# Two-layer decoder with 64 routed experts: meta sums behind gate and up, shorter gathered rows, token lists handed out in two parts

## What is computed

```
scores  = sigmoid(x @ w_router)                      # 272 x 64
groups  = the best 4 of 8, by their two best biased scores
top_idx = the 8 best experts of those groups
gates   = scores[top_idx] / sum * 2.5
routed  = sum over the chosen experts e of gate * ((silu(x @ w_gate[e]) * (x @ w_up[e])) @ w_down[e])
shared  = (silu(x @ ws_gate) * (x @ ws_up)) @ ws_down
h       = layer_norm(alpha * h + routed + shared)
```

## Time and profile before

| | |
|---|---|
| median of 3 runs | 1403.47 us (1402.36 to 1405.37) |
| the profiled execution | 1402.51 us, its span 1400.7 us |
| PE busy | 1351.8 us (97%) |
| DVE, ACT, POOL busy | 429.9, 221.4, 350.7 us |
| DMA | 475.60 MB, mean 340 GB/s |
| chain that ended last | PE 78%, SPq 11%, DMA 4%, DVE 3% |

### The profile page before, as it was taken

One profiled execution on the slowest core, in us unless ns is written; L12 is line 12 of the kernel. 1 busy time (PEld: TensorE's weight loads), 2 busy tenths in 40 slices (PEclk: granted clock), 3 DMA queues, 4 the chain that ended last, 5 costly groups with the idle time before them and its releaser, 6 DMA issues.

```text
span 1400.7 us, 20398 instructions
## 1 busy us (share of the span) xinstructions
PE 1351.8 (97%) x7932; PEld 706.5 (50%) x7932; DVE 429.9 (31%) x1278; ACT 221.4 (16%) x547; POOL 350.7 (25%) x371
## 2 busy tenths in 40 slices
PE   8999999999999999999989999899999999999997
PEld 4755454454454454445448555455454545444443
DVE  0442562222322322222154424532223232222223
ACT  1154120101111111011021540101111011101001
POOL 2031435232232232232000212352222323222201
PEclk9999999999999999999999999999999999999999
DMA  9732378999999999999875224699999999999993
GB/s 338 309 120 78 135 252 319 423 419 419 422 422 419 422 422 422 420 421 421 339 261 192 85 99 155 253 393 420 422 418 422 421 421 419 421 422 421 420 424 153
DMA packets 92098, 475.60 MB, mean 340 GB/s; under 512 B 16292, under 2 KB 22744, under 8 KB 42752
## 3 DMA queue, kind: packets, MB, share of 16 engines
q1 hardware_dynamic: 76864, 442.73, 77.7%
q0 software_dynamic: 15168, 32.01, 6.3%
HBM read 491.21 MB, written 3.75 MB: 353 GB/s over the span
## 4 chain that ended last, share of the span: by engine, by line
PE 78%; SPq 11%; DMA 4%; DVE 3%; issue 2%; POOL 1%; ACT 1%; POOLq 0%; DVEq 0%; ACTq 0%
PE bank L636 24%; PE bank L666 13%; PE bank L613 13%; SPq L469 11%; PE bank L715 6%; PE bank L726 5%; PE bank L942 3%; DMA ring<-in_w_up_dram 2%; PE bank L837 2%; PE bank L654 1%; DMA arena<-h_rows,rank_i 1%; PE bank L609 1%; PE bank L985 1%; PE bank L818 1%; PE bank L586 1%
## 5 line engine op out<-in xcount | busy, mean ns | idle before, releaser
L1883 POOL DMA_INDIRECT arena<-h_rows,rank_i x256 | 255.7, 999 | 649.6 <-DVE arena L1551 504.9
L636 PE MATMUL bank<-ring,arena 128*64 128x256 f32 x2816 | 313.4, 379 | 12.9 <-DMA ring<-in_w_up_dram 9.4
L636 PEld LDWEIGHTS bank<-ring,arena 128*64 128x64 f32 x2816 | 203.8, 137 | 133.9 <-issue 28.0
L613 PE MATMUL bank<-arena 128*128 128x512 f32 x512 | 247.1, 606 | 0.0
L1584 DVE TENSOR_TENSOR arena<-arena,bank 128x256 f32<-128x256 f32 x64 | 26.9, 421 | 561.2 <-ACT arena L1153 561.2
L666 PE MATMUL bank<-ring,arena 128*64 128x512 f32 x704 | 160.8, 598 | 0.0
L1546 DVE STREAM_TRANSPOSE arena<-arena 128x256 f32<-128x256 f32 x256 | 141.5, 609 | 30.5 <-DMA arena<-h_rows,rank_i 27.0
L1158 ACT ACTIVATE arena<-bank 128x512 f32<-128x512 f32 x128 | 76.5, 598 | 440.4 <-PE bank L666 440.4
L636 PE MATMUL bank<-arena 128*64 128x256 f32 x1280 | 142.2, 379 | 3.8 <-DMA arena<-in_w_up_dram 3.8
L613 PEld LDWEIGHTS bank<-arena 128*128 128x128 f32 x512 | 87.7, 191 | 87.7 <-issue 86.7
L636 PEld LDWEIGHTS bank<-arena 128*64 128x64 f32 x1280 | 91.7, 137 | 59.4 <-issue 10.6
(11 more groups left out here) (213 smaller groups left out, 898.2 us busy)
## 6 DMA issues: line engine op xcount, KB each, us to landing
ring<-in_w_gate_dram SPq DMA_DIRECT2D x44, 2048.0 KB, 25.7
ring<-in_w_up_dram SPq DMA_DIRECT2D x44, 2048.0 KB, 27.8
ring<-in_w_down_dram SPq DMA_DIRECT2D x44, 2048.0 KB, 25.5
arena<-in_w_gate_dram SPq DMA_DIRECT2D x20, 2048.0 KB, 25.9
arena<-in_w_up_dram SPq DMA_DIRECT2D x20, 2048.0 KB
arena<-in_w_down_dram SPq DMA_DIRECT2D x20, 2048.0 KB, 25.6
ring<-in_w_in_dram SPq DMA_DIRECT2D x8, 2048.0 KB, 21.6
ring<-in_w_o_dram SPq DMA_DIRECT2D x4, 2048.0 KB, 11.6
```

Source lines behind the costliest of these rows:

```text
L613: last = mm(bank[SUM_BANKS[n][half]][0:w, :], selg[:, u, t0:t0 + w], y_sb[:, u, half * 512:(half + 1) * 512], start=False, stop=stop, skip ...
L636: last = mm(bank[5][64 * e:64 * e + 64, part * F:(part + 1) * F], xgT[:, u, kk, 64 * e:64 * e + 64], w[:, e, kk, :], start=(kk == 0), stop ...
L1883: pool.indirect_dma_start(out=xg[:, u, b, :], out_offset=None, in_=h_rows, in_offset=bass.IndirectOffsetOnAxis(ap=rank_i[:, at:at + 1], ax ...
```

## The change

**Meta sums.** In layer 0 the four meta matmuls of a pair stand directly behind gate and up, ahead of the three full ones.

**Rows.** The gates of even experts are stored only with quarters 0 and 1 of a token, those of odd experts only with quarters 2 and 3, which are the rows that the even and the odd blocks' masks pick from. A row is 256 + 32 = 288 numbers. The gates are kept sorted by parity, the product that makes them is two instructions, and each chunk has two stores of half the width, one issued by SP and one by ACT, ahead of ACT's second `shared_gate`. `read_gate` reads four columns instead of eight.

**Lists.** After four of the eight steps DVE copies the first half of the list, PE turns it after the first of its open sums, DVE reads the first half's row numbers after the sixth step, and POOL gathers pair 0's blocks 0 and 2; the second half follows as before, with blocks 1 and 3. Pair 0's rows arrive on two semaphores of their own. SP waits for the second of them before the last slot. The two semaphores come free because the w_o loads count on `w_in_in`.

```diff
-ROW = QUARTER + E
+ROW = QUARTER + PAIRS
 XG = 4 * ROW
...
+        def store_gates(eng, n, e):
+            t0, w = CHUNKS[n]
+            eng.dma_start(h_quads[t0:t0 + w, 2 * e:2 * e + 2, QUARTER:ROW],
+                          gates[0:w, n, e, :].unsqueeze(1).to_broadcast([w, 2, PAIRS])).then_inc(gates_stored, 16)
...
                 for n in QUERIES[l]:
-                    t0, w = CHUNKS[n]
-                    sp.dma_start(h_quads[t0:t0 + w, :, QUARTER:ROW], gates[0:w, n, :].unsqueeze(1).to_broadcast([w, 4, E]))\
-                        .then_inc(gates_stored, 16)
+                    store_gates(sp, n, 0)
...
-                sp.wait_ge(gathered[0][l], 64)
+                sp.wait_ge(first_rows_in[1], l * 32 + 32)
...
                         pe.wait_ge(selg_ready[l], r * 32 + p)
+                        if l == 0:
+                            scatter(l, 1 - u, 0, 0)
                         scatter(l, 1 - u, 1, 0)
                         scatter(l, 1 - u, 1, 1)
                         scatter(l, 1 - u, 2, 0)
-                        if l == 0:
-                            scatter(l, 1 - u, 0, 0)
...
-                open_sums(1)
+                open_sums(1, (0,))
+                pe.wait_ge(score_ready, SCORED[l])
+                if l == 0:
+                    pe.wait_ge(shared_sig, SHARED[l][0])
+                hold_here(pe, quads_ready[l], 1)
+                turn_list_half(0).then_inc(list_turned[l], 1)
+                open_sums(1, (1,))
                 last = open_sums(2)
...
-                turn_lists(l, 0)
+                hold_here(pe, quads_ready[l], 2)
+                turn_list_rest().then_inc(list_turned[l], 1)
...
                 shared_gate(1)
+                act.wait_ge(gates_ready, l + 1)
+                for n in QUERIES[l]:
+                    store_gates(act, n, 1)
                 shared_gate(2)
...
+                    if j in (3, 7):
+                        dve.tensor_copy(quads[:, j // 4, :, :], list_halves[:, j // 4, :].unsqueeze(1).to_broadcast([64, 4, 32]))\
+                            .then_inc(quads_ready[l], 1)
+                    if j == 5:
+                        dve.wait_ge(list_turned[l], 1)
+                        dve.tensor_scalar(ids[:, :, 0, :], turned_ids[:, :, 0, :], -4.0, k["quarter"], ALU.mult, ALU.add)\
+                            .then_inc(ids_ready[l], 1)
...
+                def first_turned():
+                    for half in range(2):
+                        dve.wait_ge(first_rows_in[half], l * 32 + 32)
+                        for e in range(2):
+                            last = turn_block(0, 2 * e + half)
+                    last.then_inc(xt_ready[l], 1)
...
-                step(dve.tensor_tensor(part["tmp"], part["score"], part["chosen"], ALU.mult))
+                for e in range(2):
+                    step(dve.tensor_tensor(part["tmp"][:, :, PAIRS * e:PAIRS * e + PAIRS], by_parity["score"][:, :, e, :],
+                                           by_parity["chosen"][:, :, e, :], ALU.mult))
...
+                    if q == 0 and not extra:
+                        for half in range(2):
+                            hold_here(pool, ids_ready[l], half + 1)
+                            for e in range(2):
+                                gather(0, 2 * e + half, first_rows_in[half])
+                        continue
```

More of the change, by code:

```diff
@@ L155, in shape_constants @@
     c["tri"] = np.tile((np.arange(8)[None, :] < np.arange(8)[:, None]).reshape(1, 64), (128, 1))
-    c["half"] = np.stack([(p // 32 == b) & (p // 64 == e) for b in range(4) for e in range(2)], axis=1)
+    c["own"] = np.stack([p // 32 == b for b in range(4)], axis=1)
     c["quarter"] = (4 * FAR + p // 32)[:, None]
@@ L412, in decoder_kernel @@
         gather_over = per_layer("gather_over")
+        first_rows_in = [sem(f"first_rows_in{half}") for half in range(2)]
         out_ready = sem("out_ready")
@@ L592, in features_ready, with turn_list_half, turn_list_rest, turn_lists @@
                 pe.wait_ge(hT_dve, FEATURE_DVE[event][n])
-            def turn_lists(l, r):
-                hold_here(pe, quads_ready[l], r + 1)
-                own = ident[0:64, 0:64].rearrange("p (q e) -> p e q", e=2)
+            own = ident[0:64, 0:64].rearrange("p (q e) -> p e q", e=2)
+            def turn_list_half(half):
+                for e in range(2):
+                    b = 2 * e + half
+                    last = mm(bank[7][:, PAIRS * (b + 1):PAIRS * (b + 2)], mo["quads"][0:64, 128 * half:128 * half + 128],
+                              own[:, e, :], start=True, stop=True)
+                return last
+            def turn_list_rest():
                 for e in range(2):
                     mm(bank[7][64 * e:64 * e + 64, 0:PAIRS], mo["list"][0:64, :], own[:, e, :], start=True, stop=True)
[L600 to L603, removed]
+                return turn_list_half(1)
+            def turn_lists(l, r):
+                hold_here(pe, quads_ready[l], r + 2)
+                turn_list_half(0)
+                turn_list_rest().then_inc(list_turned[l], 1)
             def scatter(l, u, n, half, stop=False):
@@ L1038, in open_sums @@
                     else:
-                        for half, b in enumerate(SUM_BANKS[n]):
+                        for half in halves:
+                            b = SUM_BANKS[n][half]
                             last = mm(bank[b][:, :], k["alpha"], h_tok[:, n, half * 512:(half + 1) * 512], start=True, stop=False,
@@ L1512, in make_lists @@
                     hold_here(dve, list_step[l], r * (CAP // 4) + 2 * j + 2)
+            quads = mo["quads"][0:64, :].rearrange("p (h q s) -> p h q s", h=2, q=4)
+            list_halves = mo["list"][0:64, :].rearrange("p (h s) -> p h s", h=2)
+            ids = rank_i[:, :].rearrange("p (e h q) -> p e h q", e=2, h=2)
+            turned_ids = bank[7][:, PAIRS:5 * PAIRS].rearrange("p (e h q) -> p e h q", e=2, h=2)
             def first_lists(l):
@@ L1567, in round_ @@
                     dve.wait_ge(gu_done[l], r * 32)
-                turned(0, 0, 1, first=True)
+                if extra:
+                    turned(0, 0, 0, first=True)
+                else:
+                    first_turned()
                 read_gate(0, 0)
@@ L1575, in two_pairs @@
                         if not (final and u == 1):
-                            turned(p + 1, 1 - u, i + u + 1, first=first and u == 0)
+                            turned(p + 1, 1 - u, i + 1, first=first and u == 0)
                             read_gate(p + 1, 1 - u)
```

85 lines of the change are left out of this document (44 added, 41 removed).

## The result

The kernel became slower: median **1413.37 us** (five runs, 1409.30 to 1417.46) against 1405.12 (1402.36 to 1405.45) of the kernel before in the same measurement, ratio 1.0062, 95% interval 1.0045 to 1.0078. The forecast was 1394.1, and even the range, up to 1400.0, missed it. Lines are now those of the changed kernel: gate/up L652 (before L636), meta sums L625 (L609), full sums L629 (L613), down L682 (L666), shared expert L1072 (L1055), DVE's turns of the gathered rows L1578 (L1546), gathers L1926 (L1883).

The account below looks back on a forecast made before the run. PE (78% of the span) was taken as the bound, with weight transfers close behind. Gains of 4.7 us in each layer took 1402.5 to 1393.1; 1.0 more for the median gave 1394.1 us, range 1389.5 to 1400.0.

Parts of the forecast that it names:

- Part 1: Layer 0's pairs, meta sums behind gate and up: PE 0.21 us less a pair, 6.5 us over 31 pairs.
- The cap by the weights: End of layer 0: up weights come only 3.7 us earlier, slack 0.8, so three of 6.5 us are lost.
- Part 2: Gathers with rows of 288 instead of 320 numbers: 0.08 us a pair, 2.4 us a layer where weights bind.
- the sum: Whole kernel: 4.7 us gained in each layer, 9.4 together, for a median of 1394.1 us.
- short rows don't shorten the transfers: Rival on the gathers: engine time goes by row, not byte; no gain from short rows, 1398.9 us; chance 0.17.
- Part 3: Start of each layer's pairs, lists in two parts: pair 0 starts 1.3 us earlier in layer 0, 2.3 in layer 1.
- Edits at nothing: Split gate stores, product as two instructions, less zeroing, other w_o semaphores: off the path or hidden, priced at nothing.
- tell-tales: Signs in the profile: layer 0 pairs 14.91 us, q0's share 5.4 to 5.6%, layer 1's starved pairs 16.0 us.
- The rival on the slower side: Layer 0's switch from gate/up to narrow tiles exposes small weight loads; at 0.65 us a switch, 1408.0 us; chance 0.04.
- The waits for up weights in layer 1: PE over layer 1's pairs: 9.4 us in 8 waits, said to be of the ring's slots alone.

Follow-up runs that it names:

- e10: The kernel before with only the meta sums moved ahead of the full ones: 1399.02 us, ratio 0.9976.
- e1: The change with four unused numbers behind the constants, so the arena begins at byte 127,488 again, as before: 1394.53 us, ratio 0.993.
- e4: The change without short rows (320 numbers, all 64 gates, eight read), arena at 127,488: 1392.81 us, ratio 0.9922.
- e9: e4 with ring and arena on multiples of 512 bytes: 1385.62 us, ratio 0.9875.
- e12: e1 with ring and arena on multiples of 512 bytes, so with short rows: 1381.56 us, ratio 0.9853.
- e15: e9 repeated on another chip: 1396.99 us, ratio 0.9925.
- e16: e12 repeated on another chip, together with e15: 1394.74 us, ratio 0.9907.
- e2: The kernel before with only its arena 32 bytes further, at 127,520: 1415.53 us, ratio 1.0095.
- e11: e4 with the meta sums back behind the full ones, leaving lists in two parts and the split store alone: 1395.18 us, ratio 0.9952.
- e5: e1 with the buffer of gathered rows alone 32 bytes further, slots in place: 1395.96 us, ratio 0.9953.
- e7: e1 with the buffer of gathered rows alone 64 bytes further, slots in place: 1395.98 us, ratio 0.9954.
- e13: e1 with the gathered rows alone 120 numbers, 480 bytes, further, slots in place: 1411.69 us, ratio 1.0032.
- e18: e1 once more, on a further chip beside a repeat of the change: 1403.39 us, ratio 0.9983.

## Why the forecast was wrong

- **Part 1 (meta sums)**: right on PE, 14.91 us a pair. Its yield was put at 1.0 us and measured 3.4 (1.7 to 5.0) in e10. The cap by the weights was right in kind: in e1 PE waits for up weights at the end of layer 0, 2.8 us in three waits, as foretold (2 to 3).
- **Part 2 (short rows)**: the sum's term was 2.4 us a layer; e1 against e4 (0.993 and 0.9922) shows none. The gathers did get cheaper (5.6% in e1 on the same 1344 packets, 6.0% before: 0.06 us a starved pair, 0.08 forecast), but the step took it as given that the saved time goes to the weights at their old speed. They lost it again: 319 ns a packet near a gather in e1, 314 in e4. The rival "short rows don't shorten the transfers" had the right term for the wrong reason. And the term hangs on placement: on multiples of 512 the same shortening brought 4.1 us (e9 to e12) and 2.3 us (e15 to e16), against 4.8 in the sum, neither clear of the intervals.
- **Part 3 (lists)**: put at 3.6 us without part 2, measured 6.7 (5.0 to 8.6). Pair 0 of layer 0 started as forecast in the change's trace, but traces differ: it starts at 213.0 to 218.2 us in the 17 with lists in two parts (mean 216.1) and at 215.3 to 218.7 in the three without (before, e2 and e10; mean 217.1). From layer 0's pair 31 to layer 1's pair 0 it is 216.6 to 221.8 us in the 17 (mean 219.8) and 222.8 to 224.1 in the three (mean 223.6). That is 1.1 us for the forecast 1.3, and 3.8 for 2.3. Pair 0 of layer 0 itself, which had taken 16.5 us before, takes 15.9 in e11. The rest I have not taken apart.
- **The failed step** is a term that the sum did not have. "Edits at nothing" names the stores, the product, the zeroing and the semaphores, but not the size of the constants' table. The shorter table moved slots and rows, the weights came at 412 instead of 419 GB/s, and the price was 14 to 19 us, one and a half times to twice the whole forecast gain of 9.4 (the 19 has 2.3 us of the gaps in pair 0, which the change's trace has and e1's has not). Without it the change gives 1394.5 us beside 1402.9, next to the forecast's 1394.1, but that is luck: parts 1 and 3 gained 3.4 and 6.7 us where 1.0 and 3.6 were forecast, and part 2 cost about 1 where it was to gain 4.8.
- The forecast's tell-tales worked: q0's share of 5.7% missed the foretold 5.4 to 5.6, and starved pairs were 16.2 us where 16.0 had been forecast (16.1 before). The rival on the slower side, and the only one, was the wrong mechanism: the switch behind gate/up costs nothing that can be seen (7.01 us as before).
- Two slips in the prediction change nothing in its sum. The waits for up weights in layer 1 are not of the ring's slots alone: the same view of the kernel before has 3.8 us in three waits for the arena's. And the 206.2 and 207.3 us of part 3 are 906.2 and 907.3.

**A rule that was weighed for one end only.** The rows first: 426 GB/s with ring, arena and the buffer of long rows beginning on multiples of 512 (its rows then lie on multiples of 256), 425 with short rows there; 421 with the ring 128 bytes behind one; 419 with short rows besides; 416 with the slots 32 bytes ahead of a multiple or with the rows at 480; 412 with both. The Trainium skill, DMA: Bandwidth & Descriptors, section "How a descriptor splits into AXI transactions", lets every transaction start on a multiple of 256 bytes; the bytes ahead of the start are fetched unused and still cost beats of 32 bytes. The forecast used that for the rows in device memory only. Taken over to the place of arrival, which the page does not name, the rule makes 8192 bytes at 128 behind a multiple cost 260 beats instead of 256, by which 309.2 ns would become an estimated 314.0; the trace has 314.2 in the ring, away from gathers. For the short rows it gives 38, 39, 40 and 41 beats on average at 0, 32, 64 and 480 bytes, and the runs fall in the same order: 419, 418, 418, 416 GB/s.

It fails in three places, so these agreements don't prove it. At 32 behind a multiple (e2) 257 beats would be an estimated 310.4 ns, and the slots' packets took 315.5. One half of one slot, the odd expert's up weights in the arena, begins 192 bytes behind a multiple of 512 even in e9; 262 beats would be an estimated 316.5 ns, but of the up weights' packets into the arena, half of which go there, 97% took at most 310 ns. And the rows' own packets of 4608 bytes took 183.3 ns in e1, e5 and e7 alike and 184.2 in e13, where 39, 40 and 41 beats instead of 38 would add 3 to 8%; what a bad place slows is the weight packets beside them, of which the rule says nothing. Why a place is bad stays open.

## What to carry to other kernels

A kernel whose DMA engines are full has a term for where each buffer begins: print the byte at which ring, slots and gathered rows start, before and after a change, and try multiples of 512 for large destinations by ordering the allocations. Here the step from e4 to e9 was worth some 7 us (ratios 0.9922 and 0.9875, read on two chips), and the slide by 32 bytes cost 14 to 19. That 512 is the unit is not shown: 32 bytes off was bad on either side and 128 behind was too, while 192 behind was not; for the slots 256 was not tried. When a change shortens a table, suspect the place of what is allocated behind it. Where the DMA share stays at 1.0, compare GB/s: the share can't tell full and fast from full and slow.

The best kernel found is e12, the change with ring and arena on multiples of 512: 1.5% faster than the kernel before on one chip (0.9831 to 0.9875), 0.9% on another (0.9882 to 0.9931).

## What the runs showed that I had not expected

- 32 bytes of displacement of one tile cost 0.95% of a kernel that was otherwise unchanged (e2).
- The price of a place shows in the packets of others: with the gathered rows at 480 bytes, weight packets within half a microsecond of one took 329 ns instead of 319 (e13, e1); on multiples of 512 with 1280-byte rows the difference near a gather is gone (309.2 and 309.2, e9).
- Pair 0 of layer 0 takes 15.9 us in the ten kernels of e1 to e12 that have the lists in two parts and 17.6 in the two that don't (e2 and e10, where PE waits 2.63 us for the rows and is granted 0.50 to 0.56 of its clock over 3 us of the row). In e13 to e18, on two other chips, it takes 21.2 to 25.3, with idle stretches of up to 1.0 us inside PE's row that the profile puts down to "issue". Two profiles of one kernel (e9 and e15) differ mainly there: 15.9 and 24.5 us, spans of 1386.8 and 1394.3. The kernel before took 2 to 5 us more on these chips, e9's kernel 11. Why, and whether the kernel before has these gaps there too, stays open: its runs there show times only.
